# Filter sums on TensorE, eight modulation units moved, attention bias on VectorE, in a two-block transformer kernel

## The reference

```python
mod = c_act @ ada_w[l] + ada_b[l]                    # 6 * 2048 sums over 2048
sh1, sc1, g1, sh2, sc2, g2 = jnp.split(mod, 6, axis=-1)

# every attention: a bias by distance, per head, before the softmax
bias = tab.astype(jnp.float32)[:, :, t5_bucket(jnp.asarray(rel * dist_scale))]
s = jnp.einsum('bhgnqd,bhnkd->bhgnqk', qb, kb) * SCALE + bias[None, :, :, None]

# Hyena filters of the second block
h = jnp.sin(fr * (h @ w3 + b3))                      # the last of three layers
h = (h @ w4).reshape(L, N_DIR, HYENA_ORDER, D_HYENA) * decay
k = jnp.concatenate([h_fwd, zeros(1), h_bwd[:0:-1]], axis=0)
k = k / jnp.sum(jnp.abs(k), axis=0, keepdims=True)
return jnp.fft.rfft(k, axis=0)                       # 257 frequencies
```

## Time and profile before

| | us |
|---|---|
| median of 3 runs | 3005.53 |
| lowest, highest | 2999.02, 3006.77 |
| the profiled execution | 2999.47 |
| its span | 2997.7 |
| VectorE busy from 66 to 182 us (the front's blocks) | 114.80 of 116 |
| TensorE busy in the same stretch | 74.48 |
| TensorE busy from 560 to 678 us (attention stage 4) | 117.45 of 118 |
| TensorE busy from 678 to 2997 us | 2189.93 of 2319 |

### The profile page before, as it was taken

How to read it: one execution, slowest core, us unless ns; L and a number is a source line. 1 busy time by engine, 2 the same in 40 slices (tenths; PEclk the granted TensorE clock), 3 DMA queues, 4 the chain that set the end, 5 groups by cost and what they waited for, 6 DMA issues and landing times.

```text
span 2997.7 us, 36656 instructions
## 1 busy us (share of the span) xinstructions
PE 2752.5 (92%) x14444; PEld 2296.5 (77%) x14444; DVE 1880.2 (63%) x2345; ACT 1278.0 (43%) x1540; POOL 24.4 (1%) x46
## 2 busy tenths in 40 slices
PE   3769999897999999999699898999899999999997
PEld 0258898676788787877499396999778888888886
DVE  6986665566666788898766444444555455445444
ACT  2024543342444577777433053534344444443443
POOL 0000000000000000000000000000000000000000
PEclk9789998797999999999899997999999999999999
DMA  8787674340777899999444252544355655555553
GB/s 326 297 319 262 245 272 165 109 173 33 254 258 248 292 324 370 368 369 370 162 168 169 83 190 89 183 177 182 140 196 168 193 187 194 187 195 190 189 197 112
DMA packets 178526, 644.87 MB, mean 215 GB/s; under 512 B 10923, under 2 KB 10988, under 8 KB 134104
## 3 DMA queue, kind: packets, MB, share of 16 engines
q1 hardware_dynamic: 170208, 593.53, 55.7%
q0 software_dynamic: 5344, 30.93, 2.8%
q10 hardware_dynamic: 2840, 18.56, 1.7%
HBM read 635.59 MB, written 7.39 MB: 214 GB/s over the span
## 4 chain that ended last, share of the span: by engine, by line
PE 73%; DVE 12%; DMA 8%; ACT 3%; issue 2%; DVEq 0%; ACTq 0%; SPq 0%
PE ps L1570 72%; DMA raw<-in_stream 7%; DVE w_lo L914 3%; DVE raw L993 2%; ACT w_hi L579 2%; DVE arena L975 0%; DVE arena L973 0%; DVE arena L1073 0%; DVE arena L1089 0%; DVE arena L1475 0%; DVE h_lo L965 0%; PE ps L1704 0%; DVE arena L1473 0%; DVE arena L1474 0%; PE ps L2061 0%
## 5 line engine op out<-in xcount | busy, mean ns | idle before, releaser
L914 DVE TENSOR_TENSOR w_lo<-raw,w_hi 128x1024 fp32r<-128x1024 f32 x968 | 1171.4, 1224 | 803.6 <-ACT w_hi L579 801.0
L579 ACT ACTIVATE w_hi<-raw 128x1024 fp32r<-128x1024 f32 x968 | 1011.8, 1057 | 946.3 <-PE ps L1570 853.2
L1570 PE MATMUL ps<-w_hi,h_hi 128*128 128x512 f32 x1216 | 477.0, 392 | 16.2 <-DVE h_lo L1529 10.0
L1570 PE MATMUL ps<-w_hi,r_hi 128*128 128x512 f32 x1184 | 469.2, 396 | 13.9 <-DVE w_lo L914 5.7
L1570 PE MATMUL ps<-w_lo,h_hi 128*128 128x512 f32 x1216 | 475.0, 391 | 0.0
L1570 PE MATMUL ps<-w_hi,h_lo 128*128 128x512 f32 x1216 | 475.0, 391 | 0.0
L1570 PE MATMUL ps<-w_hi,r_lo 128*128 128x512 f32 x1184 | 462.8, 391 | 0.0
L1570 PE MATMUL ps<-w_lo,r_hi 128*128 128x512 f32 x1184 | 462.8, 391 | 0.0
L1570 PE MATMUL ps<-h_hi,w_hi 128*128 128x256 f32 x1536 | 441.6, 287 | 11.5 <-DVE h_lo L965 3.9
L1570 PE MATMUL ps<-h_lo,w_hi 128*128 128x256 f32 x1536 | 438.1, 285 | 0.0
L1570 PE MATMUL ps<-h_hi,w_lo 128*128 128x256 f32 x1536 | 437.9, 285 | 0.0
(11 more groups left out here) (270 smaller groups left out, 1898.1 us busy)
## 6 DMA issues: line engine op xcount, KB each, us to landing
raw<-in_stream SPq DMA_DIRECT2D x524, 1024.0 KB, 5.5
under_r<-in_stream SPq DMA_DIRECT2D x80, 512.0 KB, 5.2
arena<-in_mod_units ACTq DMA_DIRECT2D x16, 1024.0 KB, 4.8
filters<-arena POOLq DMA_DIRECT2D x4, 1280.0 KB, 5.3
arena<-filters POOLq DMA_DIRECT2D x4, 1280.0 KB, 6.0
x<-in_x POOLq DMA_DIRECT2D x1, 2048.0 KB, 19.7
arena<-bias_rows POOLq DMA_DIRECT2D x2, 1024.0 KB, 6.3
x<-bias_rows POOLq DMA_DIRECT2D x2, 1024.0 KB, 10.5
```

The lines of the kernel that those rows point to most:

```text
L579: act.activation(dst, src, ACT.Copy).then_inc(hi_ready, 1)
L914: dve.tensor_tensor(low, src, high, ALU.subtract).then_inc(lo_ready, 1)
L1570: return pe.matmul(o, a, b, start=start, stop=stop)
```

## The change

Three parts.

1. The front. The backward taps' first row is cleared at the source: ScalarE copies the third layer's output with a zero first column, and `make_taps` uses that copy for one of its four products. The spectrum takes the taps themselves, forward and backward, with a third table of negated sines: 20 products for 10. `taps_norm` swaps its operands, so that the sum of a channel stands in the channel's partition: 16 products with one column for 4 with 512. The reciprocal is then 128 x 4. To bring it back over all partitions, ScalarE multiplies the identity by each of its four columns, TensorE multiplies ones by these (`norm_spread`), and ScalarE copies the result.
2. `FIRST_UNITS` is 32. A block of the front carries five units, and the half units number 96. `ASIDE` gives five of six steps one half unit (before, two of three), the steps of stages 1 to 3 have 11 for 8, and the gap at step 71 has none for 4.
3. The bias. GpSimd's queue copies the rows of a mixer 128 times within the chip's memory (`spread_rows`, 1.5 MB), and the table is loaded from there in the right order. VectorE adds it to the scores in PSUM and takes the maximum in one instruction. The two products with `flip` go.

The diff, cut to its core:

```diff
-FIRST_UNITS = 40
+FIRST_UNITS = 32
...
-        counts.append(1 if beside or k % 3 < 2 else 0)
+        counts.append((2 if k % 8 in (1, 4, 6) else 1) if beside else 1 if k % 6 else 0)
...
+            pool.wait_ge(sem("brow_stored"), 16)
+
+            def spread_rows(m):
+
+                src = bass.AP(tensor=brow.tensor, offset=8 * m * 384, ap=[[384, 8], [0, P], [1, 384]])
+                pool.dma_start(skew[m], src).then_inc(sem(f"rows_spread{m // 2}"), 16)
+            spread_rows(0)
             for b in range(4):
                 pool.wait_ge(sem("spectrum_out"), 5 * b + 5)
                 pool.dma_start(kf_dram[b], ko[b % 2].rearrange("p a n -> p (a n)")).then_inc(sem(f"kf_stored{b % 2}"), 16)
...
-            pool.wait_ge(sem("brow_stored"), 16)
+            spread_rows(2)
...
             pool.wait_ge(sem("att_out"), 16 * 2)
+            spread_rows(1)
             toeplitz(1, toep2)
             load("ld_cmp", (w1k, d["w1k"]), (w1v, d["w1v"]), (w2c, d["w2kv"]), (peT, d["pe"]))
+            spread_rows(3)
...
+                act.wait_ge(sem("rn_ready"), b + 1)
+                for q in range(4):
+                    ins = act.activation(rn_diag[:, q, :], ident, ACT.Copy, scale=rn_cols[:, q:q + 1])
+                ins.then_inc(sem("rn_act"), 1)
+                if b >= 2:
+                    act.wait_ge(sem("spectrum_out"), 5 * (b - 1))
+                act.wait_ge(sem("rn_spread"), b + 1)
+                copy(rnorm[b % 2], ps[:, 2, :]).then_inc(sem("rn_act"), 1)
...
-                ch(dve.reciprocal(rnorm[b % 2], ps[:, 2, :]))
-                for t in range(TH):
-                    for op, o in ((ALU.add, 0), (ALU.subtract, 2)):
-                        dve.tensor_tensor(taps_abs[b % 2][:, o + t, :], taps[b % 2][:, 2 * t, :], taps[b % 2][:, 2 * t + 1, :], op)\
-                            .then_inc(sem("parity_ready"), 1)
+                if b:
+                    dve.wait_ge(sem("rn_act"), 2 * b)
+                dve.reciprocal(rn_cols, ps[:, 2, 0:4]).then_inc(sem("rn_ready"), 1)
...
-                modulation(done_units + 1, 6)
-                done_units += 7
+                modulation(done_units + 1, 4)
+                done_units += 5
...
-                        dve.tensor_reduce(m[:, 0:1], ps[:, b, 0:128], AX, ALU.max, negate=True)
-                        ch(dve.tensor_reduce(m[:, 1:2], ps[:, b, 128:384], AX, ALU.max, negate=True))
+                        for col, (lo_k, width) in enumerate(((0, P), (P, T))):
+                            s = ps[:, b, lo_k:lo_k + width]
+                            ins = dve.tensor_tensor_reduce(s, s, bias[:, t % 8, T - width:T], 1.0, NEG / SCALE, ALU.add, ALU.max,
+                                                           m[:, col:col + 1])
+                        ch(ins)
...
-                for n in range(4):
-                    pe.wait_ge(sem("abs_ready"), 4 * b + n + 1)
-                    ins = mm(ps[:, 2, :], ones[:, :], taps_abs[b % 2][:, n, :], n == 0, n == 3)
+                pe.wait_ge(sem("abs_ready"), 4 * b + 4)
+                if b:
+                    pe.wait_ge(sem("rn_act"), 2 * b)
+                for q in range(4):
+                    for n in range(4):
+                        ins = mm(ps[:, 2, q:q + 1], taps_abs[b % 2][:, n, q * P:(q + 1) * P], ones[:, 0:1], n == 0, n == 3)
                 ins.then_inc(sem("norm_mm"), 1)
+
+            def norm_spread(b):
+
+                pe.wait_ge(sem("rn_act"), 2 * b + 1)
+                for q in range(4):
+                    ins = mm(ps[:, 2, q * P:(q + 1) * P], ones[:, :], rn_diag[:, q, :])
+                ins.then_inc(sem("rn_spread"), 1)
...
-                pe.wait_ge(sem("parity_ready"), 4 * b + 4)
-                for n, (m, c0, o) in enumerate(((cosm, 0, 0), (cosm, P, 0), (sinm, 0, 2), (sinm, P, 2), (nyq, 0, 0))):
+                norm_spread(b)
+                for n, (ahead, back, c0) in enumerate(((cosm, cosm, 0), (cosm, cosm, P), (sinm, minus, 0), (sinm, minus, P), (nyq, nyq, 0))):
                     for t in range(TH):
-                        ins = mm(ps[:, 3 + n, :], m[:, t, c0:c0 + P], taps_abs[b % 2][:, o + t, :], t == 0, t == 1)
+                        mm(ps[:, 3 + n, :], ahead[:, t, c0:c0 + P], taps[b % 2][:, 2 * t, :], t == 0, False)
+                        ins = mm(ps[:, 3 + n, :], back[:, t, c0:c0 + P], taps[b % 2][:, 2 * t + 1, :], False, t == 1)
...
-                        mm(ps[:, b, 0:128], q[:, 0:P], kt[:, 0:P], True, False)
-                        mm(ps[:, b, 0:128], flip, bias[:, P:T], False, True)
-                        mm(ps[:, b, 128:384], q[:, P:T], kt, True, False)
-                        mm(ps[:, b, 128:384], flip, bias, False, True).then_inc(sem("att_s"), 1)
+                        mm(ps[:, b, 0:128], q[:, 0:P], kt[:, 0:P])
+                        mm(ps[:, b, 128:384], q[:, P:T], kt).then_inc(sem("att_s"), 1)
```

68 lines of the change are left out of this document (38 added, 30 removed).

## The result

The changed kernel takes 3031.99 us (median of 4 runs, 3031.29 to 3036.77), the kernel before 3004.93 on the same chip. The ratio is 1.0107, with a 95% interval from 1.0096 to 1.0119: slower by 27 us. The forecast was 3000, and 3018 was the upper end of its range.

A forecast was written before the change was run, and what follows sets the result against it. After the change TensorE bounds the front, transfers the projections, the VectorE-ScalarE ring the first attention stages. Front -8.3, stage 4 -14 and its entry -1.9, against lateness and slower heads, sum to -5.5 us: 3000 us, range 2978 to 3018.

The forecast's parts named there:

- the moved units: Half units moved into projections and attention stages: lateness of +3.5 us before stage 1, +1.5 before stage 2, +4 before stage 3.
- the allowance for the clock: Front: time added for TensorE running at its lower clock, 3 us in the first block and 1.5 in each other.
- The heads: Attention stages 1 and 2: a head's mean step grows to 6.31 us, +2.9 a stage; stage 3, +1.9.
- the ring: Attention heads: VectorE and ScalarE steps following each other, from maxima to next maxima, half unit included; mean step 5.83 us before.
- the 1 us added for close half units: Attention stages 1 and 2: +1 us each for half units that follow each other within 6 us.
- The entry to stage 4: Start of the last attention stage: the slow entry gets 1.9 us shorter.
- stage 4 at -11.7 against -14: Last attention stage, 16 heads in pairs: 1.75 us saved a pair, -14 us in all (-8 to -17).
- The reduction with the add: Maxima on VectorE in each head: adding the bias there costs +0.05 us a head, between 0 and +0.4.
- the fourth rival: Attention heads: the reduction with add costs +0.4 us a head in 40 heads, time 3014; chance 0.09.
- The front (-8.3 against +0.5): Front: TensorE sets the blocks, 25.0 us each at full clock; the front ends at 172.8 against 181.1, -8.3 us.
- The first rival: Front: the clock holds because TensorE has no pause left; front -17.5 us, time 2991; chance 0.20.
- The third rival: Projections: half units land every 3.8 to 4.0 us, not every 3.5; sum +11.5, time 3017; chance 0.20.

The follow-up runs named there:

- wide_sums: The changed kernel with the sums of the absolute taps given 128 equal columns in place of one, same count of passes; 3012.40 us against 3002.05 for the kernel before.
- light_loads: The changed kernel with most half units' loads cut to an eighth of their bytes and their product scaled by zero; 3007.27 us against 3002.05 for the kernel before.
- units_back: The changed kernel with its second part undone (40 front units, 80 half units, old table); 2994.61 us against 3000.09 for the kernel before.
- bias_only: The kernel before with the third part alone: bias added by VectorE, spread copies, no flip products; 2989.98 us, ratio 0.9968.
- bias_early: The kernel before with the third part alone and all four spread copies in the front; 2991.15 us against 3002.05 for the kernel before.

## Why the prediction was wrong

Of the 33.3 us between the sum (-5.5) and the traces (+27.8), 19.5 lie between the stages (the moved units and the copies), 8.8 in the front (the allowance for the clock), 2.7 in the heads of the first three stages and 2.3 in stage 4.

**The bound of the kernel in each stretch** was read rightly, and so was that TensorE takes the front over. The heads came out close (6.33 against 6.31 us, +4.2 and +4.4 against +3.9 each), in part by luck: I set the 6.31 against TensorE's one step of 5.95, while the eight heads before took 5.73 on average, so that the growth of the ring alone gives these 4 us and the 1 us added for close half units was not needed. The entry to stage 4 came out exactly, stage 4 at -11.7 against -14: a pair takes 12.6 us, which was my price for the ring, but it is TensorE alone that fills it (I had 12.3 for TensorE), and a pair before took 14.1 on average, not the 14.4 of the one I read. The reduction with the add costs 0.11 us a head against the 0.05 taken; the fourth rival is out.

**The front (-8.3 against +0.5)** failed in one term. The prices of the passes were nearly right: 3.63 and 6.98 us for the thin sums (3.6 and 6.9), 25.6 us for a block at full clock (25.0). What was mis-sized is the allowance for the clock: 3 us for the first block and 1.5 for each other, 7.5 in all. Behind the thin sums, taps and spread run at the lower clock and the start of the spectrum too: against the blocks of wide_sums (24.8, 25.6, 25.6 and 23.5 us, the first from the end of the sums), those of the changed kernel (30.4, 30.4, 28.7 and 26.0) are longer by 5.7, 4.7, 3.1 and 2.6, 16.0 in all. That is 8.5 us more than allowed, nearly the whole miss of 8.8. I had written that TensorE without a pause need not hold the clock, from one row, and then priced half of what followed from it. (The row itself stands behind a pause of 5.22 us, so it didn't show that thin passes bring a fall.) The Trainium skill, page TensorE: Matmul & The Clock Gate, part 1, says that activity releases the throttle. As the prediction read it, a TensorE that never stops holds 2.4 GHz; the changed kernel's trace speaks against that reading, with TensorE busy for 30.00 of 30 us and the clock at 0.83 on average, while wide_sums, where it stays at 1.00, fits it. The first rival's front (-17.5) is nearly what wide_sums has (-14.5): it needed one changed size. Its 66.0 us for the end of the first sums at full clock doesn't follow from the terms given (60.2 + 3.6 + 0.6 = 64.4), and even in wide_sums these sums took 6.72 us and ended at 67.1.

**The moved units** are the step that decided. Between the stages I had +3.5, +1.5 and +4, and it was +9.2, +6.0 and +13.3. The sum went by bandwidth (2.1 MB more, 6 us, less 3.6 of spare time; it took 350 GB/s as the upper rate of such stretches, where the earlier trace rows has 325 and 331). What the trace shows in place of it is the interval of the landings: 3.84 us in the first projections, for the 3.4 to 3.5 that the sum needed, and VectorE waits for one landing after the other. light_loads shows that the transfers are the cause (+0.5 at stage 1 in place of +9.7). The third rival had this mechanism, and 13 + 5 + 8 = 26 us of lateness against 28.5 measured. That the two sums are so close is partly luck: the moved units make 21.1 of it (8.6 + 5.6 + 6.9, by units_back), and copies, which the rival didn't have, most of the rest. Its 3017 was credited with a gain of the front and with more of stage 4; with the measured front (+8.8) and stage 4 (+2.3) it becomes 3028. It had a chance of 0.20 because I took it that half units would land every 3.5 us, and the only row I had said 3.8 to 4.0.

**The copies.** Of the 13.3 us in the third projections about 6.4 belong to the spread copies (units_back; 6.3 in light_loads). I had put copies and three half units into the same +4. In units_back the first copy does no harm in the front; that all four would do none, as I thought for bias_early, was wrong.

**Open.** Whether a half unit is late because only two places take the landings, because it stands behind weights on SP's queue, or because the DMA engines have little time left (busy share 0.88 in the first projections, 0.85 from 430 to 500 us in the third), no run separates; a third place was not tried. How much of a head's 6.33 us comes from TensorE's lower clock in stage 1 (0.85 on average) is open too. And why the clock falls behind one-column passes no run shows; shown is only that it does, and that with 128 columns it doesn't.

## What to carry to other kernels

When work is taken from the engine that bounds a stage, ask of each part of it what the next bound is: here 11 us less per block on VectorE were worth nothing because TensorE's added products filled the same time, and the units that left with them had to be paid for elsewhere. A place with spare engine time has to have spare transfer time as well: read the DMA share and the waits for landings, and take the interval at which such loads already land there (3.8 to 4.0 us before, 3.84 after) rather than bytes over bandwidth. Before a summation is moved to TensorE as one-column products, look at the granted clock behind them; wider ones took the same time.

## What the runs showed of the hardware

- 32 f32 passes with one column took 3.63 us at the higher clock, with 128 columns 3.73. Behind the one-column ones the clock fell to 1.2 GHz in three blocks of the changed kernel, for 10.2, 6.8 and 6.8 us; at the first two falls TensorE had not been idle, at the third it paused for 1.6 us. Behind the wide ones of wide_sums it did not fall, over the same pause.
- The clock column reads 1.00 for 58 to 66 us of the changed kernel, while the same passes take 6.98 us: the trace's first record of the clock stands at 78 us, ahead of it the column is not a measurement, and there the passes' own length is the better sign of the level.
- A VectorE reduction that adds a second operand and writes back to PSUM cost 0.11 us more than two plain reductions over the same 128 and 256 elements.
- A copy of 1.5 MB within the chip's memory took 19.0 to 23.5 us (medians of light_loads and units_back) to land in the third projections, and beside two of them half units of 0.5 MB landed in 7.7 us (bias_only), without them in 5.4 (bias_early).
